# Two transposes of the first mixer's sixth head, moved between steps of the output projection

## The reference, cut to what matters

```python
s = jnp.einsum('bhld,bhsd->bhls', qb, kb) * w_intra
num = jnp.einsum('bhls,bhsv->bhlv', s, vb) + w_inter[..., None] * jnp.einsum('bhvd,bhld->bhlv', c_prev, qb)
den = jnp.sum(s, axis=-1) + w_inter * jnp.einsum('bhd,bhld->bhl', n_prev, qb)
hb = num / jnp.maximum(jnp.abs(den), jnp.exp(-m))[..., None]
...
y = from_blocks(hs).astype(u.dtype) * jax.nn.sigmoid(og)
return y @ w_out
```

## Time and profile before

| what | us |
|---|---|
| median of 3 executions | 815.05 |
| lowest, highest | 814.75, 815.78 |
| the profiled execution, its own time | 816.1 |
| its span in the trace | 814.3 |
| PE busy in the span | 801.9 |
| DVE, ACT, POOL busy | 592.0, 417.1, 144.2 |

### The profile page before, as it was taken

How to read it: one execution, slowest core, us unless ns; L and a number is a source line. 1 busy time by engine, 2 the same in 40 slices (tenths; PEclk the granted TensorE clock), 3 DMA queues, 4 the chain that set the end, 5 groups by cost and what they waited for, 6 DMA issues and landing times.

```text
span 814.3 us, 15551 instructions
## 1 busy us (share of the span) xinstructions
PE 801.9 (98%) x6350; PEld 775.7 (95%) x6350; DVE 592.0 (73%) x958; ACT 417.1 (51%) x710; POOL 144.2 (18%) x156
## 2 busy tenths in 40 slices
PE   9999999999999999999999999999999999999997
PEld 9999999999899999999999999999899999999986
DVE  6777766798687875788777779976667567567753
ACT  7544444445267565555444455436555454555541
POOL 3800000032220000020000004230245302035510
PEclk9999999999999999999999999999999999999999
DMA  9876776686336643458867779535544651744531
GB/s 335 302 257 220 237 251 237 217 298 191 104 118 207 197 122 101 155 178 291 282 230 261 253 231 341 184 105 207 153 158 129 183 161 47 258 156 131 155 104 52
DMA packets 45191, 158.84 MB, mean 195 GB/s; under 512 B 5040, under 2 KB 6576, under 8 KB 45120
## 3 DMA queue, kind: packets, MB, share of 16 engines
q1 hardware_dynamic: 45120, 157.85, 58.5%
HBM read 156.76 MB, written 1.06 MB: 194 GB/s over the span
## 4 chain that ended last, share of the span: by engine, by line
PE 80%; DVE 11%; ACT 5%; issue 3%; POOL 1%; DVEq 0%; POOLq 0%; ACTq 0%
PE ps L110 72%; PE ps L112 8%; DVE w L112 3%; ACT w L112 2%; DVE u L112 2%; DVE tmp L112 1%; DVE yg L112 1%; DVE cv L112 1%; ACT SW L112 1%; ACT L112 1%; ACT ytm L112 1%; POOL rst L112 1%; DVE Vs L112 0%; DVE g L112 0%; POOL hT L112 0%
## 5 line engine op out<-in xcount | busy, mean ns | idle before, releaser
L110 PE MATMUL ps<-u,w 128*128 128x256 f32 (+1 forms) x3887 | 502.1, 285 | 2.8 <-ACT u L112 0.8
L110 PEld LDWEIGHTS ps<-u,w 128*128 128x128 f32 x3887 | 483.0, 189 | 12.2 <-issue 2.8
L112 DVE TENSOR_TENSOR w<-raw,w 128x1024 fp32r<-128x1024 f32 x245 | 297.5, 1226 | 141.9 <-ACT w L112 141.5
L112 ACT CAST w<-raw 128x1024 fp32r<-128x1024 f32 x245 | 254.0, 1048 | 127.3 <-PE ps L112 121.8
L110 PE MATMUL ps<-h,w 128*128 128x272 f32 (+1 forms) x1000 | 130.0, 285 | 0.0
L110 PEld LDWEIGHTS ps<-h,w 128*128 128x128 f32 x1000 | 125.7, 188 | 0.1
L112 POOL TENSOR_TENSOR sqa<-sqa,sq 128x272 f32<-128x272 f32 (+1 forms) x16 | 20.7, 1294 | 322.4 <-ACT sq L112 322.0
L112 POOL TENSOR_SCALAR Sb<-Sb,st 128x256 f32<-128x256 f32 x32 | 45.0, 1424 | 89.1 <-DVE st L112 89.1
L112 DVE SCALAR_TENSOR_TENSOR acc<-adr,cact,acc 128x1024 f32<-128x1024 f32 x42 | 57.7, 1398 | 0.0
L112 ACT ACTIVATE si<-tmp 128x272 f32<-128x272 f32 (+1 forms) x44 | 18.7, 424 | 70.0 <-DVE tmp L112 70.0
L112 PE MATMUL ps<-u,w 128*128 128x256 f32 (+1 forms) x169 | 48.1, 285 | 0.0
(11 more groups left out here) (185 smaller groups left out, 746.8 us busy)
## 6 DMA issues: line engine op xcount, KB each, us to landing
raw<-wst SPq DMA_DIRECT2D x245, 512.0 KB, 4.6
adr<-wada SPq DMA_DIRECT2D x48, 512.0 KB, 4.1
Bt<-bias_rows SPq DMA_DIRECT2D x8, 192.0 KB
hT<-xT SPq DMA_DIRECT2D x4, 272.0 KB, 5.4
outT<-yg SPq DMA_DIRECT2D x4, 256.0 KB, 2.1
cs<-cst SPq DMA_DIRECT2D x1, 140.0 KB, 5.3
cs<-cst SPq DMA_DIRECT2D x1, 128.0 KB, 7.2
vc<-vec SPq DMA_DIRECT2D x1, 101.0 KB, 3.6
```

Of the source, the lines that this page charges most:

```text
L110: fn()
L112: fn().then_inc(m[0], m[1])
```

## The change

`output(NH - 3)`, that is `output(5)`, is no longer called between the loop over heads and the output projection. It is called by `hook(1)`, behind the 9 matmuls of step 0, and `output(6)` and `output(7)` stay at `hook(2)` and `hook(4)`.

```diff
             sums_over_keys(h)
             if h % 2 == 0 and h < NH - 2:
                 weights(h // 2 + 1)
-        output(NH - 3)
         ustate["use"] = swr[3]
         ygm = {}
 
         def last_outputs(i):
-            if i in (2, 4):
-                output(5 + i // 2)
+            if i in (1, 2, 4):
+                output((5, 6, 7)[i // 2])
             elif i == 5:
                 low_y()
```

## The result

The changed kernel takes 817.99 us (median of 6 executions, 817.69 to 819.51) against 814.91 for the kernel before (6 executions, 814.67 to 815.78): a ratio of 1.0038, 95% interval 1.0028 to 1.0048. It is slower by 3.1 us. Forecast were 818.05 in the range 816.1 to 818.9, that is +3.0.

What follows compares the result with a forecast made beforehand. PE was taken to bound the kernel, busy 801.9 of 814.3 us. A wait of +1.5 us and a clock fall of +1.5 us, added to the median 815.05, gave 818.05, in the range 816.1 to 818.9.

Steps and rivals of the forecast that it cites:

- The removed wait: At the seam, PE's 0.62 us wait for ytm goes; PE is ready for head 6's transposes 0.78 us earlier.
- rival B: At head 6's transposes, no wait: head 5's og done by 317.50, the whole 0.78 us gained, 814.3; chance 0.05.
- What holds head 6's transposes: Bank 6 waits for head 5's og, on DVE behind the fifth chunk's split; transposes start at 319.72, a 2.2 us wait.
- The size of the wait: +1.44 us at head 6's transposes plus 0.06 for the restart: +1.5 us for PE's stream from step 2 on.
- What is late next: After head 6's transposes: head 7's transposes have no wait; low parts for steps 4, 5 and 7 are ready in time.
- The clock: Behind the 2.2 us wait, PE's granted clock falls to 0.50 for some 3.4 us, costing 1.5 us, or 0.
- Rival A: At head 6's transposes, the wait alone with the clock staying up: +1.5 us, 816.55; chance 0.28.
- The span of the profiled execution: Whole kernel: the same sum added to the profiled execution's span of 814.3 gives 817.3.

Runs made afterwards that it cites:

- the version with the split behind: Changed kernel with the fifth chunk's split asked for at step 5's hook, behind the outputs of heads 6 and 7: 814.18 us against 814.99 for the kernel before.
- own bank: Changed kernel with head 5's transposes written to PSUM bank 4 instead of 6, all queues in the same order: 814.69 us against 814.99 for the kernel before.
- transposes at the seam: Changed kernel with head 5's transposes back before step 0, the fifth chunk's split still ahead of head 5's og: 816.25 us against 814.99 for the kernel before.
- 16 fillers: Changed kernel with 16 unused matmuls of 256 columns ahead of head 6's transposes: 816.30 us against 814.99 for the kernel before.
- the 1.32 and 1.75 us above: Pauses left in the changed kernel with 8 or 4 filler matmuls ahead of head 6's transposes: 816.91 and 816.99 us against 815.19 for the kernel before.

## Why the prediction was right, step by step

**The removed wait.** Right. Step 0 starts at 314.37 and its own wait costs nothing. PE would have been ready for head 6's transposes 0.8 us earlier than before, counted from the last sums; the version with the split behind shows 0.84, where 0.78 was forecast. Its new time of 814.18 is the 814.3 of rival B, reached by another edit than the one under test.

**What holds head 6's transposes.** Right, and the step on which the sign hung. The chain ran as worked out: cast where `y1[5]` had started, 1.07 to the subtraction (1.09 forecast), 1.14 to `og`. The own bank showed that bank 6 is the link, and the transposes at the seam that the split's place makes the wait, not the place of the transposes.

**The size of the wait.** 1.58 at head 6's transposes against 1.44, and 0.04 for the restart against 0.06: 1.62 against 1.5. Two small terms were off. The `ytm` row started 0.06 later relative to the sums (314.48 against 315.05 - 0.63). And PE followed DVE's `og` by 0.15 us (319.08 to 319.23), where I had taken the 0.05 by which it had followed ACT.

**What is late next.** Right for the changed kernel: head 7's transposes and steps 4 to 7 wait for nothing. The sum left out head 4's `y2` between the two `og`, which cost nothing there, since the transposes of head 6 came later than it ended, but it made the expectation for the own bank 0.3 us too low.

**The clock.** Right in kind and in size: 1.53 us by the landmarks of the two traces, 1.7 by the medians with and without 16 fillers, 1.5 forecast from six filler matmuls at either clock. The section of the Trainium skill that I had set against it ("TensorE: Matmul & The Clock Gate", "HAM oscillation — how this bites in real kernels") warns only of longer gaps; here a gap of 2.27 us was enough in both traces of the changed kernel, so the measurement decides against taking it as a safe bound. Rival A, the wait without the fall, is what the fillers and the transposes at the seam show on purpose (816.3), and at most one of the eleven executions of the changed kernel, the one at 816.68; that one has no trace, so it is not shown to be one.

One premise of rival A was luck of the one trace then at hand. There the clock stayed up through the pause of 1.06 us at 217. With the same pause, 1.07 and 1.06 us behind a few narrow matmuls, it fell in the trace of the changed kernel (at 218.0) and in the one with the transposes at the seam (at 217.8), and stayed up in seven of the ten traces (in the tenth, with the split behind, it fell ahead of the pause, at 216.6). So neither outcome at one pause is a promise for the next execution, and the 1.32 and 1.75 us above, with one trace each, are no safe bounds.

**What was only nearly right.** The span of the profiled execution was forecast at 817.3 and is 816.0. The step that fails there is adding a difference to one execution's span while its own falls at 344.6 and 675.7, and the moment when the clock first rises, change from execution to execution. For the median the same sum holds to 0.1.

## What to carry to other kernels

When a step is moved later in a program that is written queue by queue, look at what the move lets pass in front of it on every engine, not only on the one that waited: here a weight split that had no hurry came to stand between a PSUM bank and its reader. Then follow the bank or buffer that the moved step releases to its next writer; a second bank takes the loss away, and the unhurried work moved behind keeps the gain. And price a pause of TensorE such as this one (2.27 us) twice, once for the wait and once for the fall of the clock that may follow it. When two kernels are compared by one trace each, measure from a landmark just ahead of the change to one just behind it: here the spans differed by 1.7 us, the seam by 3.15 and the medians by 3.1.

## What the runs showed of the hardware that I had not expected

- How long PE takes to follow DVE depended on the releasing instruction. It is 0.15 us from the end of DVE's `og`, which reads a PSUM bank, to the transposes (319.08 to 319.23; with the own bank 319.79 to 319.94), against 0.05 us from the end of ACT's `ytm` (315.82 to 315.87 before). The trace of before had both values for DVE alone. The first pair has a releaser that reads PSUM (`tmp<-ps,tmp`, 359.45 to 359.60), the second has one that does not (`w<-raw,w`, 554.93 to 554.98):

```profile
359.03 0.42 DVE L112 TENSOR_TENSOR tmp<-ps,tmp 128x256 f32<-128x256 f32 x1
359.60 0.59 PE L110 MATMUL ps<-u,w 128*128 128x256 f32 x3 [0.41 <-DVE tmp L112]
```

```profile
553.70 1.23 DVE L112 TENSOR_TENSOR w<-raw,w 128x1024 fp32r<-128x1024 f32 x1 [1.16 <-ACT w L112]
554.98 0.74 PE L110 MATMUL ps<-u,w 128*128 128x256 f32 x4 [0.44 <-DVE w L112]
```

  That PSUM makes the difference is not shown, only that these pairs fall this way; the first would have given the forecast its 0.15.
- Idle time on TensorE was cheaper when it was cut: 0.72 and 1.35 us with 18 matmuls between them left the clock at 1.00, where 2.27 us in one piece brought it to 0.50 for 3.4 us and cost 1.5 us more. Sixteen matmuls that compute nothing, put into the pause, give that back (817.99 to 816.30). In each of these cases it is one or two traces.
